# Between the two sublayers of a decoder layer: five weight buffers in place of three, more tiles split by token halves, and the norm weights multiplied on VectorE

## What is computed

```python
h = h + rms_norm(mixed @ w_out[l], ln_mix_post[l])      # w_out: 1024 x 1024
n = rms_norm(h, ln_ff_pre[l])
f = jnp.square(jax.nn.relu(n @ w_ff1[l])) @ w_ff2[l]    # w_ff1: 1024 x 4096
h = h + rms_norm(f, ln_ff_post[l])
```

## Time and profile before

| What | Value |
|---|---|
| Median of 3 runs | 1395.21 us (1392.79 to 1397.09) |
| Profiled execution | 1393.79 us, its span 1392.0 us |
| TensorE busy | 1366.7 us, 98% of the span |
| VectorE, ScalarE, GpSimd busy | 774.4 us (56%), 483.3 us (35%), 199.7 us (14%) |
| Mean granted clock of TensorE | 0.991 |
| Chain that ended last | TensorE 91%, VectorE 7%, ScalarE 1% |
| Transfers | 143.14 MB, mean 103 GB/s |

### The profile page before, as it was taken

The page is one execution under the profiler, slowest core; times in us unless marked ns, Lnnn a source line. Parts: engine busy times, 40 slices in busy tenths (PEclk is TensorE's granted clock), DMA queues, the critical chain, the costliest instruction groups (busy, mean ns, idle before and its releaser), DMA issues.

```text
span 1392.0 us, 24486 instructions
## 1 busy us (share of the span) xinstructions
PE 1366.7 (98%) x10516; PEld 1132.3 (81%) x10516; DVE 774.4 (56%) x1277; ACT 483.3 (35%) x778; POOL 199.7 (14%) x140
## 2 busy tenths in 40 slices
PE   8899999999999999999999999999899999999998
PEld 8689887887888888888788878888888888888886
DVE  6796227844765957679544634553455522355333
ACT  5354433433534435435344222112433212222231
POOL 1112000020000200002001322232322200022010
PEclk9999999999999999999999999999989999999998
DMA  5154322222222221232222466645213232223331
GB/s 212 61 174 140 107 69 91 84 70 70 68 71 89 92 70 60 64 106 69 86 77 92 152 211 184 194 137 183 75 47 106 91 100 97 92 91 92 90 91 60
DMA packets 46434, 143.14 MB, mean 103 GB/s; under 512 B 4944, under 2 KB 7416, under 8 KB 46328
## 3 DMA queue, kind: packets, MB, share of 16 engines
q1 hardware_dynamic: 46328, 141.59, 31.8%
HBM read 126.88 MB, written 16.27 MB: 103 GB/s over the span
## 4 chain that ended last, share of the span: by engine, by line
PE 91%; DVE 7%; ACT 1%; issue 1%; DMA 1%; SPq 0%; DVEq 0%; ACTq 0%
PE acc L1713 25%; PE acc L1715 24%; PE acc L1714 24%; PE ps_d L1867 2%; PE ps_a L1788 2%; PE ps_a L1799 1%; DVE w_lo L1296 1%; PE ps_d L1829 1%; DVE conv_y L1398 1%; PE ps_a L1778 1%; PE ps_a L1767 1%; PE ps_d L1839 1%; PE ps_d L1843 1%; PE ps_d L1845 1%; PE ps_a L1794 1%
## 5 line engine op out<-in xcount | busy, mean ns | idle before, releaser
L1713 PE MATMUL acc<-n_hi,w_hi 128*128 128x512 f32 (+1 forms) x984 | 395.6, 402 | 3.8 <-DVE n_lo L1586 2.4
L1715 PE MATMUL acc<-n_hi,w_lo 128*128 128x512 f32 (+1 forms) x984 | 382.2, 388 | 0.0
L1714 PE MATMUL acc<-n_lo,w_hi 128*128 128x512 f32 (+1 forms) x984 | 381.9, 388 | 0.0
L1296 DVE TENSOR_TENSOR w_lo<-w_raw,w_hi 128x1024 fp32r<-128x1024 f32 x200 | 284.6, 1430 | 147.8 <-ACT w_hi L998 147.0
L998 ACT CAST w_hi<-w_raw 128x1024 fp32r<-128x1024 f32 x200 | 209.6, 1049 | 437.8 <-PE acc L1715 437.6
L1713 PEld LDWEIGHTS acc<-n_hi,w_hi 128*128 128x128 f32 x984 | 186.7, 190 | 44.5 <-issue 5.1
L1715 PEld LDWEIGHTS acc<-n_hi,w_lo 128*128 128x128 f32 x984 | 186.5, 189 | 40.5
L1714 PEld LDWEIGHTS acc<-n_lo,w_hi 128*128 128x128 f32 x984 | 187.1, 190 | 35.1 <-issue 0.5
L1715 PE MATMUL acc<-h_hi,w_lo 128*128 128x512 f32 x256 | 101.0, 395 | 0.0
L1713 PE MATMUL acc<-h_hi,w_hi 128*128 128x512 f32 x256 | 101.0, 395 | 0.0
L1714 PE MATMUL acc<-h_lo,w_hi 128*128 128x512 f32 x256 | 101.0, 395 | 0.0
(11 more groups left out here) (336 smaller groups left out, 1933.1 us busy)
## 6 DMA issues: line engine op xcount, KB each, us to landing
w_raw<-weights SPq DMA_DIRECT2D x200, 512.0 KB, 3.6
gate_scratch<-gate_st SPq DMA_DIRECT2D x24, 256.0 KB, 2.9
g_in<-gate_scratch SPq DMA_DIRECT2D x24, 256.0 KB, 4.0
y_raw<-y_scratch SPq DMA_DIRECT2D x16, 256.0 KB, 3.7
x_tok<-x SPq DMA_DIRECT2D x4, 512.0 KB, 5.5
y_scratch<-y_st SPq DMA_DIRECT2D x4, 512.0 KB, 3.1
y_scratch<-d_ET SPq DMA_DIRECT2D x4, 512.0 KB, 3.8
y_scratch<-y_st SPq DMA_DIRECT2D x8, 256.0 KB, 2.4
```

What stands on the lines that cost most here:

```text
L1296: V_.tensor_tensor(w_lo[:, t % SPL], w_raw[:, t % RAW], w_hi[:, t % SPL].bitcast(F32), ALU.subtract).then_inc(lo_ready, 1)
L1713: mm(bank, wh, hi_of(k), start=start and k == 0, stop=False)
L1714: mm(bank, wh, lo_of(k), start=False, stop=False)
L1715: last = mm(bank, wl, hi_of(k), start=False, stop=stop and k == KT - 1)
```

## The change

It does the following, all of it between the sublayers save the number of buffers, which holds from there to the end.

- Two more buffers `wx_hi`, `wx_lo` for split weights, so five from the `out` tile number 3 on (`WIDE` = 5, `hi_of_tile`, `split_after`). The raw buffers stay three.
- `H` = 5: five `out` tiles by token halves; `HF` = 4: four `f1` tiles by token halves.
- `gain_row` moves from GpSimd to VectorE.
- The transposes of row blocks 0 and 1 (`row_back`) stand ahead of `transpose_f` of blocks 2 and 3; other banks (`back`, `result_bank`).
- Another order of splits, squares and scales on ScalarE and VectorE; SyncE's queue loads four weight tiles ahead of `h1` and `post`.

The core of the diff, in the order of the file: the buffers, SyncE's queue, `between` of ScalarE, `gain_row` of VectorE, `between` of TensorE.

```diff
-RAW, SPL = 3, 3
+RAW, SPL, WIDE = 3, 3, 5
...
+        def split_after(r):
+            t0, k = LATE[r][1:]
+            n = SPL if r < N_BR else WIDE
+            a = t0 + n if r != N_BR else T_WIDE
+            return range(a, min(t0 + k + n, NT))
...
-        H = 3
+        H, HF = 5, 4
...
-        from_f, back = (lambda i: trio[i % 3]), (lambda i: trio[(i + 1) % 3])
+        from_f, back = (lambda i: trio[i % 3]), (lambda i: trio[(0, 1, 1, 0)[i]])
...
-                if r == N_BR + 2:
+                if r == N_BR:
                     sp.wait_ge(tile_used, tiles_of(N_BR))
                     sp.wait_ge(mxl_ready, KT)
+                    for t in range(t0 + RAW + 1, t0 + RAW + WIDE):
+                        load(t)
+                    sp.dma_start(h1[:], x.rearrange("(t p) d -> p t d", p=P)).then_inc(in_h1, 16)
                     sp.dma_start(post[:], post_g).then_inc(in_post, 16)
-                    sp.dma_start(h1[:], x.rearrange("(t p) d -> p t d", p=P)).then_inc(in_h1, 16)
+                elif r > N_BR:
+                    for j in range(k):
+                        load(t0 + j + RAW + WIDE - 1)
...
                 split_hi(T_F1)
-                for e in range(KT + 1, len(OUT_PARTS) - 1):
-                    out_part(e)
-                square_row(0)
+                out_part(KT + 1)
+                for i in range(2):
+                    square_row(i)
+                out_part(KT + 2)
                 split_hi(T_F1 + 1)
-                out_part(len(OUT_PARTS) - 1)
-                square_row(1)
-                split_hi(T_F1 + 2)
                 for i in range(2):
                     scale_row(i)
+                split_hi(T_F1 + 2)
+                for e in range(KT + 3, len(OUT_PARTS)):
+                    out_part(e)
                 for i in range(2):
                     row_hi2(i)
+                split_hi(T_F1 + 3)
                 for i in range(2, ST):
                     square_row(i)
+                split_hi(T_F1 + 4)
...
+            def gain_row(i):
+                dve.wait_ge(in_post, 16)
+                if i >= 2:
+                    dve.wait_ge(tr2, i - 1)
+                dve.wait_ge(h1_ok, i + 1)
+                V_.tensor_tensor(rows[:, i % 2], h1[:, i], post[:], ALU.mult).then_inc(hg_ok, 1)
...
                 for m in range(M0 + 1, KT):
                     out_half_tile(1, m)
+                row_back(0)
+                row_back(1)
                 pe.wait_ge(o_ev, len(OUT_PARTS))
                 transpose_f(0, 2)
                 pe.wait_ge(sqs_sum, sums_before[-1])
                 pe.wait_ge(sqs_ok, len(OUT_PARTS))
                 sum_over_partitions((2, 3), ps_a[:, 2])
+                pe.wait_ge(n2l, 1)
                 transpose_f(0, 3)
-                row_back(0)
-                row_back(1)
-                for j in range(H - 1):
-                    first_f1_half(0, j)
+                first_f1_half(0, 0)
+                pe.wait_ge(h1_ok, 3)
+                first_f1_half(0, 1)
+                first_f1_half(0, 2)
                 row_back(2)
+                first_f1_half(0, 3)
                 row_back(3)
-                first_f1_half(0, H - 1)
-                for j in range(H):
+                for j in range(HF):
                     first_f1_half(1, j)
```

More of the change, by code:

```diff
@@ L728, in build, with hi_of_tile, lo_of_tile @@
         L_F2 = [48, 72]
+        T_OUT = LATE[N_BR][1]
+        T_WIDE = T_OUT + SPL
+        slot, ahead = [], []
+        for t in range(NT):
+            ahead.append(None if t < SPL or t in (T_WIDE, T_WIDE + 1) else t - (SPL if t < T_WIDE else WIDE))
+            slot.append(t if t < SPL else SPL + t - T_WIDE if ahead[t] is None else slot[ahead[t]])
+        def hi_of_tile(t):
+            return w_hi[:, slot[t]] if slot[t] < SPL else wx_hi[:, slot[t] - SPL]
+        def lo_of_tile(t):
+            return w_lo[:, slot[t]] if slot[t] < SPL else wx_lo[:, slot[t] - SPL]
+        def split_after(r):
[3 more added lines that the diff above has]
+            return range(a, min(t0 + k + n, NT))
         def tiles_of(n):
@@ L760, in result_bank @@
         def result_bank(r):
-            return ps_a[:, 2] if r in (N_BR + KT - 1, L_F1[0] + H - 1) else acc[:, r % 2]
+            if r == N_BR + KT - 1:
+                return ps_a[:, 2]
+            if L_F1[0] <= r < L_F1[0] + HF:
+                return (ps_d[:, 2], ps_a[:, 2], acc[:, 0], acc[:, 1])[r - L_F1[0]]
+            return acc[:, r % 2]
         trio = [ps_a, ps_d, acc]
-        from_f, back = (lambda i: trio[i % 3]), (lambda i: trio[(i + 1) % 3])
+        from_f, back = (lambda i: trio[i % 3]), (lambda i: trio[(0, 1, 1, 0)[i]])
         def two(ps):
@@ L856, in _ @@
             for r, (tile, t0, k) in enumerate(LATE):
-                for j in range(k):
-                    load(t0 + j + RAW + 1)
+                if r < N_BR:
+                    load(t0 + RAW + 1)
                 if r == 0:
@@ L962, in _ @@
                 if r == N_BR + KT - H:
-                    for e in range(KT - H, KT):
+                    for e in range(KT - H, len(OUT_PARTS)):
                         sum_out(e)
-                if r == N_BR + KT - 1:
-                    gain_row(1)
                 if r < N_BR and r // KT == 2:
@@ L1261, in _ @@
                 if not (tile[0] == "out" and tile[1] >= KT - H):
-                    for j in range(k):
-                        split_hi(t0 + j + SPL)
+                    for t in split_after(r):
+                        split_hi(t)
                 if r >= L_F2[1]:
@@ L1615, in _ @@
                         norm_row(0, i)
-                    split_lo(t0 + SPL + 1)
-                elif r == N_BR + KT - 1:
+                    for i in range(2):
+                        gain_row(i)
                     rms_of_rows(0)
+                    split_lo(T_F1)
+                    split_lo(T_F1 + 1)
+                    split_lo(T_F1 + 2)
+                    for i in range(2):
+                        row_lo2(i)
                     rms_of_f(2, 2, 2, ps_a[:, 2])
@@ L1622, in _ @@
                     norm_row(0, 3)
-                    for i in range(2):
-                        row_lo2(i)
-                    split_lo(t0 + SPL)
+                    for i in range(2, ST):
+                        gain_row(i)
                     rms_of_rows(1)
+                    split_lo(T_F1 + 3)
+                    split_lo(T_F1 + 4)
                     for i in range(2, ST):
                         row_lo2(i)
+                elif tile[0] == "out":
+                    pass
                 elif tile[0] == "f1":
@@ L1644, in _ @@
                         V_.tensor_tensor(f_T[:, m], f_T[:, m], bank, ALU.add).then_inc(f_ev, 1)
-                    for j in range(k):
-                        split_lo(t0 + j + SPL)
+                    for t in split_after(r):
+                        split_lo(t)
             rms_of_f(3, 0, ST, ps_d[:, 2])
```

48 lines of the change are left out of this document (21 added, 27 removed).

## The result

| | Median | Runs |
|---|---|---|
| before | 1392.95 us (1390.65 to 1397.09) | 7 |
| changed | 1385.58 us (1384.99 to 1388.61) | 7 |
| ratio | 0.9949, interval 0.9936 to 0.9962 | |

The change makes the kernel 0.51% faster: 7.4 us, where 5.85 were forecast, and the time lies 1.6 us under the lower end of the range, 1387.2. Part of that distance is in the starting point: the forecast was set on 1395.21, the median of three runs of the kernel before, and the median of seven is 1392.95, 2.3 us lower. The profiled execution of the changed kernel took 1388.61 us, the slowest of its seven; its span is 1386.8 us, 5.2 less than that of before.

A forecast was written before the change was run, and what follows sets the result against it. TensorE, busy 98%, was taken as the bound, losing 13.2 us between the sublayers before and 7.3 after; 5.85 us off the median 1395.21 gave 1389.4 us, range 1387.2 to 1393.1.

The forecast's parts named there:

- the starting point: Whole kernel: median of the runs before, 1395.21 us, from which the forecast of 1389.4 was set.
- The failed step: MLP: two more weight buffers change nothing, since TensorE waits for no weights there; costed at nothing.
- anything outside 950 to 1045 us differs: Sign that the forecast is wrong: a difference outside the part between the sublayers; no size given.
- the plan of the changed kernel: Between the sublayers: TensorE's starts written out from row durations, the fifth f1 tile at 1036.35 for 1042.20, 5.85 us less.
- the clock's fall: Rival: clock falls in the new 2.5 us gap ahead of the second halves, costing 1.2 us (1390.6) or 2.8 (1392.2); chance 0.25.
- the seven waits: TensorE's remaining waits between the sublayers: 0.4, 0.5, 0.3, 0.75, 1.4, 2.5 and 0.75, together 6.6 us.
- The product: gain_row on VectorE between the sublayers: 1.23 us each, with GpSimd's 2.85 as upper bound.
- the ReLU's wait: Ahead of the fifth f1 tile: TensorE waits 0.75 us for tile 2's ReLU, absorbing part of a clock fall.
- the more pessimistic case: Clock falls in the gap ahead of the second halves: 1390.6 us, or 1392.2 at the price seen before; chance 0.25.
- the optimistic one: Larger gain: some waits at blocks 1 and 2 vanish through overlapping instructions, 2 us more, 1387.3 us; chance 0.05.
- VectorE as the bound: Rival, between the sublayers: VectorE bounds both halves and the first row_back is late too; about 1400 us, chance 0.04.
- the rival of no change: Between the sublayers: VectorE's chain slower than planned, gain_row at 2.85 adding 3.2 us; saving 2.6, 1392.6 us; chance 0.24.

The follow-up runs named there:

- e1_wx_shift: Changed kernel with its two new weight buffers moved by 128 bytes in each partition; 1388.27 us, one execution.
- e2_w_shift: Changed kernel with the old weight buffers moved by 128 bytes and all behind them by 256; 1370.83 us, 0.9835 of before.
- e4_gain_on_pool: Changed kernel with the four products of rows and norm weights back on GpSimd; 1389.94 us, 0.9977 of before.
- e9_operand_128: Changed kernel with old weight buffers at multiples of 256 bytes, MLP operands and new weight buffers 128 bytes beyond; 1386.37 us.
- e7_al512: Changed kernel with all weights and the large products' moving operands, except the first and third branch, at multiples of 512 bytes; 1369.16 us.
- e3_rows_together: Changed kernel with row_back 3 ahead of the fourth first half of an f1 tile, not behind it; 1381.47 us, 0.9913 of before.
- the second pair: Kernel before and changed kernel, both unedited, profiled once more on one other chip; 1392.85 and 1386.35 us, one execution each.
- e5_before_w_shift: Kernel before with only w_hi and w_lo moved by 128 bytes and all behind them by 256; 1374.94 us, 0.9875 of before.
- e8_all: Changed kernel with weights and branch operands at multiples of 256 bytes and row_back 2 and 3 together; 1365.37 us, 0.9804 of before.

## Why the prediction was wrong

**The failed step** is "Two more buffers in the MLP change nothing, since TensorE waits for no weights there." The reason given is true, since no wait for weights is in either trace, and the conclusion is not: the buffers' place sets the pace of the matmuls. It was worth 2.3 us in the first pair of profiles and 3.6 in the second. The first look went past it: a busy share of 98% was read as leaving only the gaps to win, but TensorE is as busy at 5.58 us a tile as at 5.44. The prediction had named "anything outside 950 to 1045 us differs" as what would make it wrong, but gave it no price.

**The starting point** was off as well: "The median of the runs is 1395.21, so I forecast 1389.4" takes the median of three runs, and seven gave 1392.95. Of the 3.8 us between 1389.4 and the measured 1385.58, 2.3 come from there and 1.5 from the larger gain, 7.4 for 5.85. From 1392.95 the same forecast is 1387.1 and the same range 1384.9 to 1390.8, which takes in the measured time. That would have been luck: it is the sum of a stretch that gained 1.3 to 2.1 us less than planned and an MLP that gained 2.3 to 3.6 from nothing.

**Between the sublayers the plan of the changed kernel held**, up to the clock's fall. Each start less the 1.57 us by which this execution came late:

| Event | plan | measured - 1.57 |
|---|---|---|
| `row_back` 0, no wait | 1000.8 | 1000.69 |
| first `f1` half tile | 1006.2 | 1006.30 |
| second | 1009.85 | 1009.86 |
| `row_back` 2 | 1017.0 | 1016.81 |
| second halves | 1024.15 | 1023.98 |
| fifth tile, clock not fallen / fallen | 1036.35 / 1037.55 | 1037.75 |

Of the seven waits, 6.6 us by plan, 5.1 are seen: 2.4 for 2.5, 1.0 for 1.4, 0.6 for 0.75, 0.4 for 0.75, 0.4 for 0.4, 0.3 for 0.5, with `row_back` 0 without one. The 0.3 ahead of the first `f1` half tile did not appear. The starts agree all the same, since pieces behind a wait run longer than the plan took them: `transpose_f` 3 holds TensorE for 1.13 (1006.74 to 1007.87), where `row_back` 0, without a wait, holds it for 0.87 (1002.26 to 1003.13). The product was forecast at 1.23 and took it (2.47 for two).

**The clock's fall** was given 0.25 and happened. It was seen behind this wait in the changed kernel twice and in `e1_wx_shift`, `e2_w_shift`, `e4_gain_on_pool` and `e9_operand_128`, and not in `e7_al512`, which has the same wait. By the Trainium skill, page "TensorE: Matmul & The Clock Gate", section "What's actually happening", the moment isn't tied to the program; the one profile of seven without it agrees. Its price is 1.5 to 1.6 us: 101.17 against 99.68 for the stretch in `e2_w_shift` and `e7_al512`, and 1.56 in `e3_rows_together`. The prediction took 1.2, by having the ReLU's wait absorb a part. It absorbs none: that wait is 0.6 with the fall (changed) and without it (`e3_rows_together`), and 0.5 with it (`e2_w_shift`) and without it (`e7_al512`), since the second halves, whose results the ReLU waits for, are slowed as well. So the more pessimistic case held in the stretch, and the total still came out better than the optimistic one, through the MLP.

**VectorE as the bound** did not come. What a slower product costs, `e4_gain_on_pool` shows, though on GpSimd: at 2.37 each the stretch is 4.7 us longer, where the rival of no change priced 2.85 each at 3.2: it left out the wait at `row_back` 0 and a second fall of the clock. That rival also calls the row of 2.02 in place of 0.15 a two-tensor instruction; it has one tensor as input.

**Still open.** The medians differ by 7.4 us and the first pair of spans by 5.2, or 6.8 without the late start of one execution; the second pair differs by 6.5. What decides in an execution between 5.58 and 5.60 for the kernel before was not found. Nor was it found what in the memory makes the offset count. Whether the transposes ahead of the wait have a part in the clock's fall was not tried: `e3_rows_together` takes away the wait and what stands ahead of it at once.

## What to carry to other kernels

Before costing a new buffer at nothing, write down the address of both matmul operands modulo 256 bytes, before and after: an unequal offset cost 2.6% per tile here (5.58 against 5.44), 17.5 us in the whole kernel before, more than the 13.2 us lost between its sublayers. A wait that follows short transposes has two prices, its length and the fall of the clock, and a single half tile put behind the last transpose removed both. Moving a product to the faster engine and giving it cover were worth 3.8 to 4.6 us in the stretch together, but 1.0 to 2.0 and nothing apart, so such edits have to be tried as a pair. And a forecast in absolute time is no better than the median it starts from: three runs put it 2.3 us too high here.

## What was not expected of the hardware

The pitch of a full tile, 24 matmuls of 128x512 in three products, by the offsets modulo 256 bytes of weights and moving operand:

| weights / operand | pitch, us | seen in |
|---|---|---|
| 0 / 0 | 5.44 | `e2_w_shift`, `e5_before_w_shift`, `e7_al512`, `e8_all` |
| 0 / 0, beside slower tiles | 5.49, then 5.45 | new buffers of the changed kernel |
| 128 / 128, beside slower tiles | 5.49, then 5.45 | new buffers of `e9_operand_128` |
| 128 / 0 | 5.58 (5.60 in some executions) | before, old buffers of the changed kernel |
| 0 / 128 | 5.58 | old buffers of `e9_operand_128` |
| 0 / 32 | 5.60 | tiles of the first and third branch in `e2_w_shift`, `e5_before_w_shift`, `e7_al512` |
| 128 / 32 | 5.62 | the same in before and changed |
| 0 / 160 | 5.62 | the same in `e9_operand_128` |

In these runs it is the difference of the offsets that counts, 6 ns in a matmul of 227. The Trainium skill, page "SBUF — State Buffer", section "SBUF: two separate sides", says that on the engines' side only the port pair shared by VectorE and GpSimd is contended for, and that TensorE waits for no other engine. The runs agree: `e1_wx_shift` keeps the five buffers and all the work of the other engines and has lost the faster pace, so the pace follows TensorE's own two operands. Only this kernel's matmuls, fp32r of 128x512 with a weight load each, were measured.
